# Latent-attention layer of a four-layer decoder trunk: weight units dealt in another order between the softmax steps, probability products half a step later

## The chip, the cores and the metric

The kernel runs as one program on one core of a Trainium2 chip. The metric is the device time of one execution in microseconds (us), the median of several runs. PE is the tensor engine, DVE the vector engine, ACT the scalar engine, POOL the GpSimd engine, SP the engine whose queue issues all DMAs here. Each engine works through its own instructions strictly in the order in which they stand, and semaphores hold one back until another is ready.

## What is computed

A trunk of four pre-norm residual layers over 1024 tokens of width 1024: gated linear attention, latent attention, stick-breaking attention, gated linear attention. The change touches the second one alone:

```python
def mla_mixer(h, w_in, q_norm_g, kv_norm_g, w_uq, w_ukv, w_out, cos, sin):
    proj = h @ w_in
    c_q, c_kv, k_rope, g = jnp.split(proj, [...], axis=-1)
    q = (rmsnorm(c_q, q_norm_g) @ w_uq).reshape(B, S, MLA_HEADS, MLA_NOPE + MLA_ROPE)
    q_nope, q_rope = jnp.split(q, [MLA_NOPE], axis=-1)
    q_rope = apply_rope(q_rope, cos[:, None, :], sin[:, None, :])
    kv = (rmsnorm(c_kv, kv_norm_g) @ w_ukv).reshape(B, S, MLA_HEADS, MLA_NOPE + MLA_V)
    k_nope, v = jnp.split(kv, [MLA_NOPE], axis=-1)
    for i in range(S // BLOCK_Q):          # 8 blocks of 128 queries, causal
        s = q_nope @ k_nope + q_rope @ k_rope
        p = softmax(where(causal, s * scale, -inf))
        outs.append(p @ v)
    return (o * jax.nn.silu(g)) @ w_out    # 16 heads of 128
```

## The kernel before, in words

Every float32 operand is held as two float16 halves (`_hi`, `_lo`), and each product takes three matmuls.

**The list of items.** `LatentAttention.build_items` writes one list; each engine runs through all of it and does its own share of each item. So the list is the order of every engine. Sixteen heads by eight query blocks give 128 steps, t = 8 h + i; block i looks at i + 1 blocks of 128 keys, so a score row is 128 wide at i = 0 and 1024 wide at i = 7. Item `s` t is the scores on PE (it waits until the exponential of t - 2 has left its pair of PSUM banks; at i = 0 also for `stacked`, the DMAs that laid out the rotary part of the queries, `mla_qr_stack`). `m` t is the row maximum and its negative on DVE and the exponential on ACT. `d` t is the reciprocal on DVE, the scaled copy `prob_halves` (high half) on ACT, the low half on DVE, and then on SP the DMA transpose of both. `pv` t is the product with the values on PE, which waits for that transpose; after every fourth one DVE multiplies by the gate (`mla_yt`), ACT and POOL split it (`mla_y_hi`, `mla_y_lo`).

**The filling.** Between these stand the units of the next projections; a unit fills one of three accumulators (PSUM banks 5, 6, 7 in turn) and must be emptied by DVE or ACT before the third unit after it starts. In columns of 128: `qn` 24, `kn` 12, `v` 12 (two each per head, emptied by ACT and DVE; "short" units), `qr` 24 (two for each pair of heads, before the even head; three DVE instructions each), `g` 96 (two per head; ACT and DVE also compute the SiLU) and `x` 48 (four per head from head 4 on, the output projection of the four heads before; DVE adds them to the residual). `g` and `x` are cut in four parts. Item `w` is the split of a weight slab into halves: ACT `w_hi`, then DVE `w_lo`, from one of two load buffers into one of three split buffers; `finish_items` decides where it stands. Item `rope` (POOL adds, ACT `st_hi`, DVE `st_lo`) finishes a rotary unit, and the `stage` items (SP, sixteen small DMAs for a pair of heads, four in each of four steps) lay it out as `mla_qr_stack` for the next even head.

**What sets the order.** A step of the list was: `s` t+1, `pv` t-1, `m` t+1, a first gap, `d` t+1, `stage` if any, a second gap. `weave` deals the filling into the gaps in equal shares of its own cost, whatever the attention work of the step. The order of the filling of one head h is: for odd h first the `qr` slab and units of the next pair, then `qn`, `kn`, `v` of head h+1 (with `rope` behind the `qn` units), then the `x` units, then the gate `g` of head h+1. The `stage` items stand in the steps i = 3 to 6 of the main list of the odd head, which puts the last of them just behind `d` of the head's last step.

## Time and profile before

| | us |
|---|---|
| runs (3) | 2726.56, 2728.34, 2731.05; median 2728.34 |
| profiled execution | 2728.8, of it 2726.8 from the first to the last instruction |
| PE busy | 2400.1 (88%) |
| DVE busy | 1523.5 (56%) |
| ACT busy | 1325.1 (49%) |
| mean granted TensorE clock | 0.953 |

The attention steps of the latent layer lie between 601 and 1442 us. A head's first step begins where DVE's row maximum has the form 128x128, which is how the stretches below were cut. "Idle before" is the time in which an engine had nothing to run just before an instruction, and the name behind the arrow is what released it.

### The profile page before, as it was taken

Reading aid. Unit: us, or ns where it says so; the run is one execution under the profiler, and the core shown is the slowest. Engines: PE = TensorE matmul, PEld = TensorE weight load, DVE = VectorE, ACT = ScalarE, POOL = GpSimd, SP = SyncE. Lnnn points to the kernel's source line nnn. Section 1 sums busy time; section 2 is a strip of 40 time slices with the busy share of each in tenths; the row PEclk is TensorE's granted clock in tenths of the full one; section 3 lists DMA queues with packets and bytes.
Section 4 is the critical chain, followed back from the end, with each engine's and each line's share of the span. In section 5 each row is a group of like instructions: output and inputs, shape, how many; then the busy total and the mean of one; then the engine's idle time right before and its main releaser. Section 6 shows DMA issues by size and latency. Waiting matters only on the chain. (4 is left out here: it accounts for less than half of the span.)

```text
span 2726.8 us, 42519 instructions
## 1 busy us (share of the span) xinstructions
PE 2400.1 (88%) x17068; PEld 1367.7 (50%) x17068; DVE 1523.5 (56%) x2164; ACT 1325.1 (49%) x1989; POOL 358.5 (13%) x266
## 2 busy tenths in 40 slices
PE   8999988977778878888787899999999899999987
PEld 4657753434444444444453455555554345775543
DVE  5555455665455455554556566666666474546554
ACT  4432333444444444444444477777777543334332
POOL 0000001121000000000002133222333210000001
PEclk9999999998889989999899999999999899999999
DMA  3011002213333332333332211111111121101013
GB/s 110 32 40 40 32 31 85 68 37 69 70 73 70 75 78 63 71 79 69 82 73 75 62 55 55 47 55 47 47 55 32 39 86 33 40 32 40 32 54 117
DMA packets 199767, 160.27 MB, mean 59 GB/s; under 512 B 160114, under 2 KB 165490, under 8 KB 199572
## 3 DMA queue, kind: packets, MB, share of 16 engines
q1 hardware_dynamic: 199572, 157.56, 21.7%
q8 instruction: 136, 2.23, 0.3%
q14 instruction: 59, 0.48, 0.1%
HBM read 98.79 MB, written 4.19 MB: 38 GB/s over the span
## 5 line engine op out<-in xcount | busy, mean ns | idle before, releaser
L222 PE MATMUL psum<-h_hi,w_hi 128*128 128x512 f16 x1128 | 431.6, 383 | 4.1 <-PEq L647 2.7
L223 PE MATMUL psum<-h_lo,w_hi 128*128 128x512 f16 x1128 | 431.1, 382 | 0.0
L224 PE MATMUL psum<-h_hi,w_lo 128*128 128x512 f16 x1128 | 430.7, 382 | 0.0
L2226 DVE SCALAR_TENSOR_TENSOR w_lo<-wf,w_hi 128x1024 f16<-128x1024 f32 (+3 forms) x194 | 232.3, 1200 | 188.8 <-ACT w_hi L2221 188.6
L238 PE MATMUL psum<-w_hi,h_hi 128*128 128x128 f16 x1504 | 256.9, 219 | 0.0
L239 PE MATMUL psum<-w_lo,h_hi 128*128 128x128 f16 x1504 | 256.6, 219 | 0.0
L240 PE MATMUL psum<-w_hi,h_lo 128*128 128x128 f16 x1504 | 256.6, 219 | 0.0
L1079 POOL TENSOR_TENSOR sb_al<-sb_zc,sb_ah 128x256 f16<-128x256 f32 (+2 forms) x96 | 166.3, 1732 | 372.0 <-ACT sb_ah L1044 372.0
L2221 ACT ACTIVATE w_hi<-wf 128x1024 f16<-128x1024 f32 (+3 forms) x194 | 188.4, 974 | 35.2 <-PE psum L224 16.3
L1578 ACT ACTIVATE ssum<-psum,mla_neg_top 128x128 f32<-128x128 f32 (+7 forms) x128 | 94.4, 738 | 207.7 <-DVE mla_neg_top L1487 207.7
L224 PEld LDWEIGHTS psum<-h_hi,w_lo 128*128 128x128 f16 x1128 | 111.2, 99 | 135.6 <-issue 4.7
L222 PEld LDWEIGHTS psum<-h_hi,w_hi 128*128 128x128 f16 x1128 | 111.2, 99 | 123.8 <-issue 12.3
L1499 DVE SCALAR_TENSOR_TENSOR mla_prob_halves<-ssum,mla_inv_total,mla_prob_halves 128x128 f16<-128x128 f32 (+7 forms) x128 | 104.7, 818 | 120.3 <-ACT mla_prob_halves L1586 120.3
L223 PEld LDWEIGHTS psum<-h_lo,w_hi 128*128 128x128 f16 x1128 | 111.1, 99 | 119.7 <-issue 6.3
L958 DVE TENSOR_TENSOR sb_Ll<-sb_Lf,sb_Lh 128x256 f16<-128x256 f32 (+2 forms) x96 | 96.8, 1008 | 111.4 <-ACT sb_Lh L1036 111.4
L238 PEld LDWEIGHTS psum<-w_hi,h_hi 128*128 128x128 f16 x1504 | 147.1, 98 | 18.3 <-issue 12.1
L239 PEld LDWEIGHTS psum<-w_lo,h_hi 128*128 128x128 f16 x1504 | 147.2, 98 | 6.0
L1586 ACT ACTIVATE mla_prob_halves<-ssum,mla_inv_total 128x128 f16<-128x128 f32 (+7 forms) x128 | 99.1, 774 | 104.5 <-DVE mla_inv_total L1496 104.5
L240 PEld LDWEIGHTS psum<-w_hi,h_lo 128*128 128x128 f16 x1504 | 147.2, 98 | 0.0
L1403 PE MATMUL psum<-mla_prob_halves_T,mla_v_hi 128*128 128x128 f16 x576 | 112.7, 231 | 38.8 <-DMA mla_prob_halves_T<-mla_prob_halves 37.5
L1638 POOL TENSOR_TENSOR mla_y_lo<-mla_yt,mla_y_hi 128x512 f16<-128x512 f32 x32 | 36.9, 1155 | 811.0 <-ACT mla_y_hi L1595 811.0
L1483 DVE TENSOR_REDUCE mla_top<-psum 128x1 f32<-128x128 f32 (+7 forms) x128 | 96.1, 750 | 61.3 <-PE psum L1388 60.5
(295 smaller groups left out, 5624.5 us busy)
## 6 DMA issues: line engine op xcount, KB each, us to landing
wf<-in_gla_out SPq DMA_DIRECT2D x32, 512.0 KB, 3.4
wf<-in_sb_in SPq DMA_DIRECT2D x32, 512.0 KB, 3.5
wf<-in_mla_out SPq DMA_DIRECT2D x20, 512.0 KB, 3.8
wf<-in_gla_v SPq DMA_DIRECT2D x16, 512.0 KB, 3.5
wf<-in_gla_g SPq DMA_DIRECT2D x16, 512.0 KB, 3.4
wf<-in_mla_gate SPq DMA_DIRECT2D x16, 512.0 KB, 3.5
wf<-in_sb_out SPq DMA_DIRECT2D x16, 512.0 KB, 3.5
xT<-in_x_T SPq DMA_DIRECT2D x16, 256.0 KB, 5.4
```

The lines of the kernel that those rows point to most:

```text
L222: pe.matmul(out, wh[:, w], act_hi[:, k, tok], start=(i == 0), stop=False)
L223: pe.matmul(out, wh[:, w], act_lo[:, k, tok], start=False, stop=False)
L224: mm = pe.matmul(out, wl[:, w], act_hi[:, k, tok], start=False, stop=(i == last))
L238: pe.matmul(out, act_hi[:, k, tok], wh[:, w], start=(i == 0), stop=False)
L239: pe.matmul(out, act_hi[:, k, tok], wl[:, w], start=False, stop=False)
L240: mm = pe.matmul(out, act_lo[:, k, tok], wh[:, w], start=False, stop=(i == last))
L1079: pool.tensor_tensor(self.al[s % 2][:, :, off:HALF], self.zc[s % 4][:, :, off:HALF], self.ah[s % 2][:, :, off:HALF], ALU.subtract).then_in ...
L1403: pe.matmul(out, vh, hi, start=(j == 0), stop=False)
L1499: dve.scalar_tensor_tensor(out=ph[:, w:2 * w], in0=self.prob[:, 0:w], scalar=self.inv_total[:, k], in1=ph[:, 0:w], op0=ALU.mult, op1=ALU.s ...
L1586: act.activation(self.ph[t % 2][:, 0:w], self.prob[:, 0:w], ACT.Copy, scale=self.inv_total[:, t % 4:t % 4 + 1]).then_inc(self.ph_ready, 1)
L2221: act.activation(self.w_hi[s % Layer.NSPLIT][:, 0:cols], self.wf[s % Layer.NLOAD][:, 0:cols], ACT.Copy, scale=W_SCALE).then_inc(self.w_hi_ ...
L2226: dve.scalar_tensor_tensor(out=self.w_lo[s % Layer.NSPLIT][:, 0:cols], in0=self.wf[s % Layer.NLOAD][:, 0:cols], scalar=W_SCALE, in1=self.w ...
```

## The change

The same units, matmuls and elementwise instructions, in another order:

- In a step, `m` t+1 and the first gap now stand ahead of `pv` t-1: `s`, `m`, gap, `pv`, `d`, `stage`, gap.
- `weave_even` deals the filling so that attention work and filling together advance evenly over the gaps of a head; `pe_cost` now counts `s` and `pv`.
- The filling of a head is drawn from its slabs in the order of a string (`ORDER`): short units stand between the long `x` units, the `qr` units of the next pair stand in the even head among the gate's units, and their `rope` items one head later, behind the second and third unit of the odd head's filling.
- `stage` stands in the steps i = 2 to 5 of the main list, one step earlier.
- `split_early` covers all slabs from 4 on, so a `w` item stands as soon as its split buffer is free.

```diff
+def weave_even(main, filler, cost):
+
+    gaps = sum(item[1] for item in main if item[0] == "gap")
+    work = sum(cost(item) for item in main + filler)
+    out, k, weight, spent = [], 0, 0, 0
+    for item in main:
+        if item[0] != "gap":
+            out.append(item)
+            spent += cost(item)
+            continue
+        weight += item[1]
+        while k < len(filler) and spent * gaps < weight * work:
             out.append(filler[k])
             spent += cost(filler[k])
             k += 1
...
+    ORDER = "uxuxuxuuxugrgr", "uuuguugxrxxrx"
     def pe_cost(self, item):
 
+        if item[0] in ("s", "pv"):
+            return (5 if item[0] == "s" else 3) * (item[1] % TT + 1)
         if item[0] not in ("u", "part"):
             return 0
...
+        for i in order:
+            s, units = todo[i]
+            name, payload = units.pop(0)
+            out.append(L.add_unit(name, payload, s, self.ACC[len(L.units) % len(self.ACC)]))
...
+    def filling(self, h):
+
+
+        made = {}
+        if h + 1 < MLA_HEADS:
+            made["u"] = self.up_slab(h + 1)
+        if h >= self.GROUP:
+            made["x"] = self.out_slab(h // self.GROUP - 1, h % self.GROUP)
+        if 1 <= h < MLA_HEADS - 1:
+            made["g"] = self.gate_slab(h + 1)
+        if h % 2 == 0 and h + 2 < MLA_HEADS:
+            made["r"] = self.rope_slab(h // 2 + 1)
+        turns = [k for k in self.ORDER[h % self.GROUP == 0] if k in made]
+        names = sorted(made, key=turns.index)
+        items = self.add_units([made[k] for k in names], [names.index(k) for k in turns])
+        if h % 2 and h + 1 < MLA_HEADS:
+            at = [i for i, it in enumerate(items) if it[0] == "u"][1:3]
+            for c, i in reversed(list(enumerate(at))):
+                items.insert(i + 1, ("rope", 3 + h + c))
+        return items
...
-        L.split_early = range(4, 7)
+        L.split_early = range(4, 1000)
...
-                items += weave(main, L.cut(filler, ("x", "g")), self.pe_cost)
+                items += weave_even(main, L.cut(filler, ("x", "g")), self.pe_cost)
                 main, filler = [], []
-            main += [("s", t + 1)] if t < last else []
+            main += [("s", t + 1), ("m", t + 1), ("gap", 1)] if t < last else []
             main += [("pv", t - 1)] if t else []
-            main += [("m", t + 1), ("gap", 1), ("d", t + 1)] if t < last else []
-            if h % 2 and h + 1 < MLA_HEADS and 3 <= i < 7:
-                main += self.stage_items(h + 1, range(2 * i - 6, 2 * i - 4))
+            main += [("d", t + 1)] if t < last else []
+            if h % 2 and h + 1 < MLA_HEADS and 2 <= i < 6:
+                main += self.stage_items(h + 1, range(2 * i - 4, 2 * i - 2))
             main += [("gap", 1)]
```

How this moves instructions is seen at three places. First SP's queue at the end of head 5 (`prob_halves_T` is the transposed probabilities of a step, 128x16x128 that of the step with 1024 keys, `mla_qr_stack` the rotary rows of head 6, `wf` a weight load). Before:

```order
L1657 DMA_TRANSPOSE mla_prob_halves_T0<-mla_prob_halves0 128x14x128
L1670 DMA mla_qr_stack<-mla_st_hi 32x512
L1670 DMA mla_qr_stack<-mla_st_lo 32x512
L1670 DMA mla_qr_stack<-mla_st_hi 32x512
L1670 DMA mla_qr_stack<-mla_st_lo 32x512
L1657 DMA_TRANSPOSE mla_prob_halves_T1<-mla_prob_halves1 128x16x128
L1670 DMA mla_qr_stack<-mla_st_hi 32x512
L1670 DMA mla_qr_stack<-mla_st_lo 32x512
L1670 DMA mla_qr_stack<-mla_st_hi 32x512
L1670 DMA mla_qr_stack<-mla_st_lo 32x512
L2215 DMA wf0<-in_mla_q_rope 128x256
```

Now:

```order
L1704 DMA mla_qr_stack<-mla_st_lo 32x512
L1691 DMA_TRANSPOSE mla_prob_halves_T0<-mla_prob_halves0 128x14x128
L1704 DMA mla_qr_stack<-mla_st_hi 32x512
L1704 DMA mla_qr_stack<-mla_st_lo 32x512
L1704 DMA mla_qr_stack<-mla_st_hi 32x512
L1704 DMA mla_qr_stack<-mla_st_lo 32x512
L1691 DMA_TRANSPOSE mla_prob_halves_T1<-mla_prob_halves1 128x16x128
L2249 DMA wf1<-in_mla_up 128x512
```

The last four rotary DMAs have moved from behind the transpose of the head's last step to ahead of it.

Second DVE's instructions in the first step of head 5 (from the row maximum of its 128-wide block on; `mla_rt` are the products of a `qr` unit with sine and cosine). Before:

```order
L1483 TENSOR_REDUCE mla_top<-psum 128x1
L1487 TENSOR_SCALAR mla_neg_top<-mla_top 128x1
L2226 SCALAR_TENSOR_TENSOR w_lo2<-wf0,w_hi2 128x512
L1457 SCALAR_TENSOR_TENSOR mla_rt0<-psum,mla_cos 128x512
L1461 SCALAR_TENSOR_TENSOR mla_rt2<-psum,mla_sin 64x512 x2
L290 TENSOR_TENSOR mla_silu_g<-mla_silu_g,mla_gate_tmp1 128x512
L1457 SCALAR_TENSOR_TENSOR mla_rt1<-psum,mla_cos 128x512
L1461 SCALAR_TENSOR_TENSOR mla_rt3<-psum,mla_sin 64x512 x2
L1496 RECIPROCAL mla_inv_total<-mla_total 128x1
L1499 SCALAR_TENSOR_TENSOR mla_prob_halves0<-ssum,mla_inv_total,mla_prob_halves0 128x128
L2226 SCALAR_TENSOR_TENSOR w_lo0<-wf1,w_hi0 128x1024
L601 SCALAR_TENSOR_TENSOR mla_qn_lo<-psum,mla_qn_hi 128x512
```

Now:

```order
L562 SCALAR_TENSOR_TENSOR xT<-psum,xT 128x512
L2260 SCALAR_TENSOR_TENSOR w_lo0<-wf1,w_hi0 128x1024
L2260 SCALAR_TENSOR_TENSOR w_lo1<-wf0,w_hi1 128x1024
L1517 TENSOR_REDUCE mla_top<-psum 128x1
L1521 TENSOR_SCALAR mla_neg_top<-mla_top 128x1
L619 SCALAR_TENSOR_TENSOR mla_qn_lo<-psum,mla_qn_hi 128x512
L1530 RECIPROCAL mla_inv_total<-mla_total 128x1
L1533 SCALAR_TENSOR_TENSOR mla_prob_halves0<-ssum,mla_inv_total,mla_prob_halves0 128x128
L562 SCALAR_TENSOR_TENSOR xT<-psum,xT 128x512
```

The rotary products and the splits of the slabs that the next units need have left this step; two slab splits, the second of them of a slab used later, stand at the end of the step before it.

Third PE's instructions in the third step of head 5 (384 keys; `prob_halves_T` with `mla_v` is `pv`, here of one block; `mla_ckv` with `w` a short unit, `mla_y` with `w` a part of an `x` unit). Before:

```order
L1387 MATMUL psum<-mla_kr_hh,mla_qr_stack 128x384
L1388 MATMUL psum<-mla_kr_ll,mla_qr_stack 128x384
L1403 MATMUL psum<-mla_prob_halves_T0,mla_v_hi 128x128
L1404 MATMUL psum<-mla_prob_halves_T0,mla_v_lo 128x128
L1405 MATMUL psum<-mla_prob_halves_T0,mla_v_hi 128x128
L238 MATMUL psum<-w_hi2,mla_ckv_hi 128x128
```

Now:

```order
L1422 MATMUL psum<-mla_kr_ll,mla_qr_stack 128x384
L240 MATMUL psum<-mla_y_hi,w_hi0 128x512
L241 MATMUL psum<-mla_y_lo,w_hi0 128x512
L242 MATMUL psum<-mla_y_hi,w_lo0 128x512
L240 MATMUL psum<-mla_ckv_hi,w_hi2 128x512
L241 MATMUL psum<-mla_ckv_lo,w_hi2 128x512
L242 MATMUL psum<-mla_ckv_hi,w_lo2 128x512
L240 MATMUL psum<-mla_y_hi,w_hi0 128x512
L241 MATMUL psum<-mla_y_lo,w_hi0 128x512
L242 MATMUL psum<-mla_y_hi,w_lo0 128x512
L1437 MATMUL psum<-mla_prob_halves_T0,mla_v_hi 128x128
L1438 MATMUL psum<-mla_prob_halves_T0,mla_v_lo 128x128
```

Three pieces of filling now stand between the scores and the product with the values, where none stood.

## Rows read from the trace of the kernel before

**Rows 1.** Page, part 1: busy time of the engines, share of the span.

```profile
PE 2400.1 (88%) x17068; PEld 1367.7 (50%) x17068; DVE 1523.5 (56%) x2164; ACT 1325.1 (49%) x1989; POOL 358.5 (13%) x266
```

**Rows 2.** Waits of PE, 601 to 1442 us: total, times, longest.

```profile
PE psum L1382 <- DMA mla_qr_stack<-mla_st_lo: 62.0, 7, 10.4
PE psum L1403 <- DMA mla_prob_halves_T<-mla_prob_halves: 37.5, 24, 4.0
PE psum L222 <- DVE w_lo L2226: 29.6, 12, 3.7
PE psum L238 <- issue: 26.4, 8, 5.0
```

**Rows 3.** Busy time by stretch: heads 0-1, 2-3, 4-5, 6-7, 12-13, 14, 15.

```profile
core 0: us, PE busy (x) PEld busy (x) DVE busy (x) ACT busy (x) POOL busy (x), PEclk, DMA share, GB/s
601.30:693.70 92.40, 62.11 (x447) 36.28 (x446) 49.14 (x96) 43.06 (x80) 6.89 (x5) 0.87 0.37 73
693.70:793.40 99.70, 75.04 (x547) 43.48 (x546) 52.88 (x101) 47.38 (x87) 8.05 (x6) 0.89 0.34 74
793.40:906.50 113.10, 92.39 (x643) 52.76 (x642) 60.46 (x111) 49.77 (x89) 7.05 (x6) 0.92 0.34 72
906.50:1019.30 112.80, 92.31 (x643) 52.67 (x642) 60.47 (x111) 49.72 (x89) 7.05 (x6) 0.92 0.33 72
...
1244.60:1357.30 112.70, 92.33 (x644) 52.68 (x642) 60.49 (x112) 49.74 (x89) 7.05 (x6) 0.92 0.35 72
...
1357.30:1405.50 48.20, 45.61 (x340) 26.92 (x338) 27.68 (x52) 22.73 (x40) 2.31 (x2) 0.98 0.30 72
1405.50:1442.00 36.50, 26.38 (x212) 15.44 (x211) 19.31 (x41) 18.05 (x32) 2.31 (x2) 0.99 0.42 80
```

**Rows 4.** The same for head 6 alone, head 7 alone and head 0 alone.

```profile
906.50:954.80 48.30, 45.70 (x340) 26.95 (x339) 26.87 (x51) 22.10 (x40) 2.31 (x2) 0.97 0.29 58
954.80:1019.30 64.50, 46.61 (x305) 25.72 (x304) 33.60 (x61) 27.63 (x49) 4.74 (x4) 0.89 0.36 82
601.30:639.20 37.90, 22.97 (x189) 14.47 (x188) 19.71 (x43) 18.48 (x35) 1.16 (x1) 0.91 0.33 63
```

**Rows 5.** Heads 6-7, ACT's busy time: the exponential (L1578), then the scaled copy (L1586).

```profile
906.50:1019.30 112.80, 13.26 (x32) 0.92 0.33 72
...
906.50:1019.30 112.80, 12.38 (x16) 0.92 0.33 72
```

**Rows 6.** Timeline of DVE and SP's queue where head 5 ends: start, duration, [idle before].

```profile
897.88 1.28 DVE L1499 SCALAR_TENSOR_TENSOR mla_prob_halves<-ssum,mla_inv_total,mla_prob_halves 128x1024 f16<-128x1024 f32 x1 [1.22 <-ACT mla_prob_halves L1586]
...
906.52 0.29 DVE L1483 TENSOR_REDUCE mla_top<-psum 128x1 f32<-128x128 f32 x1 [6.42 <-PE psum L1388]
...
891.96 1.54 SPq L1657 DMA_TRANSPOSE mla_prob_halves_T<-mla_prob_halves  x1
...
899.20 1.98 SPq L1657 DMA_TRANSPOSE mla_prob_halves_T<-mla_prob_halves  x1
...
903.52 0.58 SPq L1670 DMA_DIRECT2D mla_qr_stack<-mla_st_lo  x1
```

**Rows 7.** Waits in head 6 (906.5 to 954.8 us) that end on PE.

```profile
DVE mla_top L1483 <- PE psum L1388: 7.1, 2, 6.4
...
ACT mla_qn_hi L594 <- PE psum L224: 2.6, 2, 1.9
...
DVE mla_yt L1509 <- PE psum L1405: 1.9, 1, 1.9
```

**Rows 8.** Timeline of DVE, first steps of head 7, and of PE, second step of head 5.

```profile
957.81 0.69 DVE L2226 SCALAR_TENSOR_TENSOR w_lo<-wf,w_hi 128x512 f16<-128x512 f32 x1 [2.50 <-ACT w_hi L2221]
...
971.31 1.07 DVE L1475 TENSOR_TENSOR mla_st_lo<-mla_rt,mla_st_hi 128x512 f16<-128x512 f32 x1 [3.29 <-ACT mla_st_hi L1568]
...
860.20 0.27 PE L238 MATMUL psum<-w_hi,mla_ckv_hi 128*128 128x128 f16 x1 [4.98 <-issue]
```

**Rows 9.** Waits of PE in head 15 (1405.5 to 1442 us).

```profile
PE psum L1403 <- DMA mla_prob_halves_T<-mla_prob_halves: 10.1, 6, 3.2
```

More of the change, by code:

```diff
@@ L1219, in add_slab @@
                 out.append(("gz", n))
-                later = [("g2", n)]
             elif name in ("qn", "kn", "v"):
@@ L1224, in add_slab @@
                 self.ropes.append((name[0], *payload))
-        return out + later
-    def gate_items(self, h):
-        return self.add_slab(self.w["gate"][h], 1024, [("g", (h, c)) for c in range(2)])
-    def head_items(self, h):
-        out = []
-        if h % 2 == 0:
-            out += self.add_slab(self.w["q_rope"][h // 2], 256, [("qr", (h // 2, c)) for c in range(2)])
-        for it in self.add_slab(self.w["up"][h], 512, [(n, (h, c)) for n in ("qn", "kn", "v") for c in range(2)]):
-            out.append(it)
-            if h % 2 == 0 and it[0] == "u":
-                name, payload = self.L.units[it[1]][:2]
-                if name == "qn":
-                    out.append(("rope", 2 + h + payload[1]))
-        return out
+        assert not any(units for _, units in todo)
@@ L1243, in stage_items @@
     def stage_items(self, h, quarters):
         return [("stage", 2 + h + i // 4, i % 4) for i in quarters]
-    def out_items(self, group, part, halves=range(2)):
-        final = group == MLA_HEADS // self.GROUP - 1
-        items = self.L.slab(self.w["out"][group * 4 + part], 1024,
-                            [("x", (2 * part + k, c, final, group)) for k in range(2) for c in halves], self.ACC)
-        self.group_end[group] = len(self.L.units)
-        return items
     def build_items(self):
```

54 lines of the change are left out of this document (33 added, 21 removed).

## The prediction

> **What bounds the kernel now.** I read the page's busy times first: PE has work for 88% of the span, DVE for 56%, ACT for 49% [rows 1]. In the latent layer that average hides two regimes, so the waits of PE come next [rows 2]. PE loses 62.0 us in seven waits for the rotary rows `mla_qr_stack`, 37.5 us for transposed probabilities, 29.6 us for `w_lo`, and 26.4 us in front of `v` units: about 155 us together. Then the stretches [rows 3]: from head 4 on a pair of heads is a pattern of 112.5 to 113.1 us that comes five times, 563.9 us in all. Inside a pair the two heads differ: head 6 takes 48.3 us, head 7 takes 64.5 us [rows 4], though PE is busy 45.7 and 46.6 us. The granted clock in a pair is 0.92, so some 8% of 112.7 us, 9 us, of PE's 92.3 us is work stretched at the lower of the two clock levels (1.2 instead of 2.4 GHz); at full rate the matmuls of a pair need 83 to 85 us. The reader is to see that PE has nearly 30 us of slack in a pair, and to ask which line of work will take it up.
>
> That line runs through DVE and ACT and is almost serial. The maximum of the next step stands on DVE behind the low half of this one, and between them ACT computes the exponential and the scaled copy while DVE waits. For a pair: DVE busy 60.5 us [rows 3], ACT's exponentials 13.3 and its copies 12.4 us [rows 5], sum 86.2 us. What else must be paid is read from head 6, the one with the fewest stalls: 26.9 us of DVE [rows 4] and half of ACT's 25.7, 12.8 us, make 39.7 of its 48.3 us. The rest, 8.6 us, is hand-overs, ACT's other work in the line, and 5.2 us in which ACT or DVE waited for PE (2.6 for a `qn` unit, 1.9 for the product behind `mla_yt`, 0.7 in `mla_top`, whose other wait of 6.4 us is that for head 6's rotary rows) [rows 7]. Without the waits for PE the rest is 3.4 us a head.
>
> **The change part by part.** Nothing is added or removed; the 60.5 us of DVE work of a pair stays 60.5 us, and so do the matmuls.
>
> *The rotary DMAs one step earlier.* In the last step of head 5 SP issues the transpose at 899.20, and only behind it the last four rotary DMAs, the last at 903.52; head 6's first maximum starts at 906.52, after DVE has stood idle 6.42 us [rows 6]. In the new order these four stand behind the transpose that was issued at 891.96 [rows 6], so they would land some 7 us earlier, about 899.3. DVE had ended the low half at 897.88 + 1.28 = 899.16 and then two gate instructions, so nothing of the 6.4 us is left. The sixteen DMAs of a pair are the same ones and keep SP just as long; they now delay the transpose behind them, which matters little since `pv` is late too. Worth: 6.4 us in each of five pairs, somewhat more in the two earlier ones (PE's seven waits are 62.0 us in all, the longest 10.4 [rows 2]). What is late next is DVE's line itself.
>
> *Short units between long ones, `w` early, rotary units in the even head.* In the first steps of head 7 DVE waits 2.50 us for `w_hi` and 3.29 us for `st_hi`, which waited for POOL, which waited for DVE's own products just before; in head 5 PE waits 4.98 us in front of a `v` unit whose accumulator these hold [rows 8]. The same pattern comes in every odd head from 5 on, and makes most of the difference of 64.5 and 48.3 us. In the new order the slab splits stand a step or more ahead, and the rotary units a head ahead of their `rope`, so each of these waits has a reason to go. The work itself does not: about 6.7 us of DVE (33.6 against 26.9 [rows 4]) that now lies in both heads.
>
> *Products half a step later.* The transpose gets half a step of filling as cover. From head 4 on PE's wait for it is about 1 us a head already; the 37.5 us [rows 2] lie in heads 0 to 3 and 15, where filling is scarce, 10.1 us of them in head 15 [rows 9]. There the gain on PE is mostly no gain in time, since DVE's line needs nearly the whole step. The cost: `mla_yt` and ACT's `mla_y_hi` now stand inside the line, ahead of the reciprocal and the copy, twice a head. A bound from below is nothing, and from above the 1.9 us wait of rows 7 for each; I take it as part of the rest below.
>
> *Steps of equal length for PE.* A full head has some 42 us of PE work, 5.2 us a step, whatever i. DVE's line is not equal: at i = 7 the copy and low half alone wait and run 1.22 + 1.28 us [rows 6], at i = 0 a few tenths. So the long steps have little spare for their share of other DVE work and PE will wait for the banks there.
>
> **The sum.** For a pair of the full kind the line takes 86.2 us plus twice the rest. With 3.4 us a head that is 93.0 us, with head 6's 8.6 us it is 103.4. The middle is 98.2; I take 99, a little above it, for the gate products inside the line and the uneven steps. Five pairs: 563.9 - 495 = 68.9 us saved. Heads 0-1, by the same rule: 49.1 + 25.7 = 74.8, plus 6.8 to 17.2, so 81.6 to 92.0, I take 87 of now 92.4: 5.4 us. Heads 2-3: 52.9 + 25.7 = 78.6, so 85.4 to 95.8, I take 90.5 of 99.7: 9.2 us. Head 14: 27.7 + 12.8 = 40.5, so 43.9 to 49.1, I take 46.5 of 48.2: 1.7 us. Head 15: now 36.5, I take 36.0: 0.5 us. Before head 0 and behind head 15 the order hardly changes: nothing. Together 85.7 us. The profiled execution took 2728.8 us, half a microsecond over the median of 2728.3; 2728.8 - 85.7 = 2643.1, against the median 2643.
>
> Ends: with every stretch at its lower bound 98.9 + 10.8 + 14.3 + 4.3 + 1.0 = 129.3 us are saved, 2599. With every one at its upper bound 46.9 + 0.4 + 3.9 - 0.9 = 50.3 us, 2678.
>
> **Rivals.** *PE becomes the bound.* If the other DVE work fits into the times in which DVE waits for ACT, a pair is bound by PE's 83 to 85 us, say 86: 133.9 us saved in five pairs, with 25 to 30 in the first four heads 2565 to 2570. For it: the DVE work alone is 60.5 us. Against it: the engines run their lists in order, and in head 6 that work stood in the line nearly in full. Chance 0.07.
>
> *Less than half.* The long steps overflow, or the rotary rows still come late, so that about 6.4 us of a pair comes back: then a pair takes 105 to 106, five save 34 to 39 us, the rest of the layer 5: about 2688. For it: two slab splits now stand together behind an i = 7 step, and with three accumulators PE stops at once when DVE is late in a run of short units. Against it: PE can be a step ahead in the scores. Chance 0.20.
>
> *Slower, by the clock.* If many small gaps replace the two large ones, the lower clock may be granted far more often. The matmuls of a pair need 84 us at full rate; at a mean clock of 0.75 they need 112, as long as now, and that is the point from which it decides; at 0.70 they need 120, 7 us more than now in five pairs and about 12 in the first heads, so near 2776. The rows speak against it: head 15 has 10.1 us of such gaps in six pieces [rows 9] and a clock of 0.99 [rows 3], head 0 is idle 15 of 37.9 us and still has 0.91 [rows 4]. A rule speaks for it: the Trainium skill, page "TensorE: Matmul & The Clock Gate", section "A second HAM failure mode: psum-queue depth-cycling", tells of a kernel that cycles through accumulator banks and idles briefly between groups of matmuls so often that the clock swings between its two rates. This kernel cycles three banks. By that rule a pair would come out at 112 or more where the sum has 99; by head 15's row the clock stays up. A second way to the same side is a wait that no row shows, of ACT for filling that PE has not yet done, with the copy queued behind it: it would have to cost 0.85 us in each of 16 steps to use up the 13.7 us of a pair. Chance of slower, both together, 0.09.
>
> **How the numbers follow.** Forecast (2599 to 2678) 0.59, less than half 0.20, PE-bound 0.07, slower 0.09, no change 0.05 (gains and losses that cancel). A measurement of this kernel can tell about 0.2%, 5.5 us, from no change. Faster by more than that: 0.59 + 0.20 + 0.07 = 0.86; within 0.05; slower 0.09. The range reaches from 2598 to 2692: it takes in the forecast's ends and most of the second case, and leaves out the PE-bound case and what is slower or the same.
>
> **What would show it.** In the changed profile no wait of PE for `mla_qr_stack` over 2 us, and no `w_lo` or `v` wait over 2 us, if these steps are right. A pair of heads at 99 us with DVE busy 60.5 us, and PE waiting in many pieces of 1 to 2 us for DVE or ACT, if the line through DVE bounds. A granted clock of 0.95 or more in a pair; under 0.85 the clock rival is at work. Heads 0 and 2 no shorter, perhaps longer than now by some 3 us (they get the `qr` units), heads 1 and 3 shorter by some 10. The forecast is wrong if a pair stays above 106 us: then I have overlooked a wait, most likely ACT's or DVE's for a filling unit in the first gap.

## The result, and the profile after

One letter has to be set right first: in the diff above, the second string of `ORDER` lacks a `u`; the kernel has `"uuuguuugxrxxrx"`.

The changed kernel takes 2665.16 us (median of four runs, 2664.72 to 2669.93), the kernel before, on the same chip, 2729.03 us (2726.56 to 2731.05). The ratio is 0.977, with a 95% interval of 0.9753 to 0.9787: some 64 us are gained. The prediction was 2643 us, in a range from 2598 to 2692. So the direction and the range held; 86 us were forecast, and a quarter of them is missing. The page after, the span and part 1:

```profile
span 2668.2 us, 42519 instructions
PE 2400.2 (90%) x17068; PEld 1361.1 (51%) x17068; DVE 1530.2 (57%) x2164; ACT 1322.1 (50%) x1989; POOL 361.3 (14%) x266
```

The work is the same [rows 1], but for 7 us more of DVE, to which the last section comes back. The span was 2726.8 us and is 58.6 us shorter. The profiled execution took 2669.9 us, 4.8 above the median of its kernel, so what the trace shows as gained is some 5 us less than the runs have. The waits of PE in the latent layer (600 to 1400 us; total, times, longest) answer [rows 2]. Lines have moved: L1416 is L1382 of before (scores), L1437 is L1403 (product with the values), L240 and L256 are L222 and L238 (units), L2260 is L2226 (`w_lo`).

```profile
PE psum L1437 <- DMA mla_prob_halves_T<-mla_prob_halves: 31.9, 23, 3.9
PE psum L1416 <- DMA mla_qr_stack<-mla_st_lo: 27.9, 7, 5.5
PE psum L240 <- issue: 13.4, 9, 2.6
PE psum L240 <- DVE w_lo L2260: 11.1, 3, 3.8
PE psum L240 <- DVE mla_kn_lo L619: 8.6, 3, 2.9
PE psum L1416 <- ACT mla_silu_g L285: 6.0, 1, 6.0
PE psum L256 <- issue: 4.5, 5, 1.2
```

The rotary rows need two corrections. One of the seven waits in their group, 3.6 us, lies ahead of head 0, where there was none before. And the 6.0 us that the view puts down to ACT stand in front of the first score of head 4:

```profile
781.89 0.26 PE L1416 MATMUL psum<-mla_kn_hi,mla_qn_hi 128*128 128x128 f16 x1 [6.04 <-ACT mla_silu_g L285]
```

That score starts 2.19 us after SP began to issue the last rotary DMA (779.70). At the six other head changes it is 2.17 to 2.23 us, so this is most likely the same wait, and ACT's instruction ended by chance in the same moment. The wait at the seven head changes has then fallen from 62.0 to 30.3 us, that for `w_lo` from 29.6 to 11.1, that in front of `v` units (L256) from 26.4 to 4.5; the one for transposed probabilities has hardly moved (37.5, now 31.9). The group `mla_kn_lo` has grown from 1.3 us. Then the stretches by pair of heads, 14 and 15 apart, cut at the same row maximum and with the same columns as in [rows 3]:

```profile
606.00:690.40 84.40, 61.56 (x452) 34.95 (x451) 49.67 (x96) 40.20 (x76) 6.62 (x5) 0.90 0.35 72
690.40:782.90 92.50, 73.98 (x545) 43.10 (x544) 54.93 (x101) 47.27 (x86) 7.83 (x6) 0.89 0.38 78
782.90:887.60 104.70, 93.19 (x643) 52.04 (x642) 61.16 (x113) 49.57 (x89) 7.84 (x6) 0.94 0.35 76
887.60:989.60 102.00, 92.38 (x641) 50.95 (x640) 60.73 (x112) 49.15 (x89) 7.84 (x6) 0.95 0.36 79
989.60:1094.90 105.30, 93.88 (x642) 52.40 (x641) 61.00 (x112) 49.37 (x89) 7.84 (x6) 0.94 0.35 77
1094.90:1195.70 100.80, 90.97 (x643) 51.26 (x642) 60.80 (x112) 49.15 (x89) 7.83 (x6) 0.97 0.38 81
1195.70:1299.90 104.20, 92.84 (x640) 52.07 (x639) 60.98 (x112) 49.37 (x89) 7.83 (x6) 0.94 0.38 82
1299.90:1347.20 47.30, 46.43 (x350) 27.00 (x349) 28.19 (x52) 24.39 (x43) 2.31 (x2) 0.99 0.41 84
1347.20:1382.70 35.50, 26.46 (x206) 15.63 (x204) 20.50 (x41) 16.50 (x30) 2.31 (x2) 0.96 0.42 93
```

This table is the result. The five pairs of the full kind took 563.9 us and take 517.0, 103.4 on average, where 99 was forecast. The term by term comparison, saved against forecast: five pairs 46.9 (68.9), heads 0-1 8.0 (5.4), heads 2-3 7.2 (9.2), head 14 0.9 (1.7), head 15 1.0 (0.5). And one term has the wrong sign: head 0 now begins at 606.0 instead of 601.3 us, 4.7 us later, where "nothing" was forecast. Together 59.3, which is the shorter span to within a microsecond.

The two heads of a pair have drawn together by less than one would think. Heads 6 and 7 took 48.3 and 64.5 us [rows 4]; now:

```profile
887.60:945.50 57.90, 54.54 (x371) 29.79 (x370) 32.88 (x61) 26.27 (x47) 5.52 (x4) 0.94 0.34 75
945.50:989.60 44.10, 37.84 (x272) 21.16 (x270) 27.84 (x52) 22.88 (x42) 2.31 (x2) 0.97 0.40 85
```

The even head has become the long one (the `qr` units and their products on DVE lie there now: 32.88 us of DVE, 54.54 of PE; DVE's share of the `rope` items stays in the odd head), and in it PE is busy for 94% of the time. That is a first sign that DVE's line is no longer alone at the bound.

**Did the rotary rows do what the sum said?** SP's queue where head 5 ends, to be read beside [rows 6]:

```profile
883.94 0.58 SPq L1704 DMA_DIRECT2D mla_qr_stack<-mla_st_lo  x1
885.59 1.73 SPq L1691 DMA_TRANSPOSE mla_prob_halves_T<-mla_prob_halves  x1
```

The last rotary DMA is issued before head 5's last transpose and not 4 us behind it. DVE and PE there:

```profile
884.28 1.28 DVE L1533 SCALAR_TENSOR_TENSOR mla_prob_halves<-ssum,mla_inv_total,mla_prob_halves 128x1024 f16<-128x1024 f32 x1 [1.22 <-ACT mla_prob_halves L1620]
885.48 1.22 DVE L2260 SCALAR_TENSOR_TENSOR w_lo<-wf,w_hi 128x1024 f16<-128x1024 f32 x1
...
887.55 0.28 DVE L1517 TENSOR_REDUCE mla_top<-psum 128x1 f32<-128x128 f32 x1
...
886.12 0.27 PE L1416 MATMUL psum<-mla_kn_hi,mla_qn_hi 128*128 128x128 f16 x1 [3.65 <-DMA mla_qr_stack<-mla_st_lo]
```

DVE goes from the low half through a slab split and two gate instructions to the first maximum of head 6 without a pause; the 6.42 us of [rows 6] are gone as forecast. But PE still stands 3.65 us before that score, up to 6.0 elsewhere, because in the changed order PE gets there sooner. On DVE that wait no longer shows; on PE it does.

### The profile page after: what moved, and what is told of

The parts are those of the page before. It is cut to its first block and busy times, and to the rows that moved or that the text cites. A ratio compares the mean times of both kernels' runs of the same rounds, so it can differ in the third digit from the quotient of the medians.

```text
span 2668.2 us, 42519 instructions
## 1 busy us (share of the span) xinstructions
PE 2400.2 (90%) x17068; PEld 1361.1 (51%) x17068; DVE 1530.2 (57%) x2164; ACT 1322.1 (50%) x1989; POOL 361.3 (14%) x266
## 5 line engine op out<-in xcount | busy, mean ns | idle before, releaser
L240 PE MATMUL psum<-h_hi,w_hi 128*128 128x512 f16 x1128 | 433.3, 384 | 11.3 <-DVE mla_kn_lo L619 8.6
L2260 DVE SCALAR_TENSOR_TENSOR w_lo<-wf,w_hi 128x1024 f16<-128x1024 f32 (+3 forms) x194 | 232.5, 1205 | 155.5 <-ACT w_hi L2255 155.2
L256 PE MATMUL psum<-w_hi,h_hi 128*128 128x128 f16 x1504 | 256.9, 219 | 0.0
L1533 DVE SCALAR_TENSOR_TENSOR mla_prob_halves<-ssum,mla_inv_total,mla_prob_halves 128x128 f16<-128x128 f32 (+7 forms) x128 | 116.4, 910 | 121.6 <-ACT mla_prob_halves L1620 121.6
L240 PEld LDWEIGHTS psum<-h_hi,w_hi 128*128 128x128 f16 x1128 | 111.5, 99 | 128.7 <-issue 20.7
L256 PEld LDWEIGHTS psum<-w_hi,h_hi 128*128 128x128 f16 x1504 | 147.1, 98 | 18.3 <-issue 12.1
L1437 PE MATMUL psum<-mla_prob_halves_T,mla_v_hi 128*128 128x128 f16 x576 | 110.5, 228 | 35.3 <-DMA mla_prob_halves_T<-mla_prob_halves 31.9
L1039 ACT ACTIVATE sb_Lf<-sb_zc 128x256 f32<-128x256 f32 (+2 forms) x96 | 80.8, 842 | 95.2 <-DVE sb_zc L970 95.2
```

Source lines behind the costliest of these rows:

```text
L240: pe.matmul(out, wh[:, w], act_hi[:, k, tok], start=(i == 0), stop=False)
L256: pe.matmul(out, act_hi[:, k, tok], wh[:, w], start=(i == 0), stop=False)
L1437: pe.matmul(out, vh, hi, start=(j == 0), stop=False)
L1533: dve.scalar_tensor_tensor(out=ph[:, w:2 * w], in0=self.prob[:, 0:w], scalar=self.inv_total[:, k], in1=ph[:, 0:w], op0=ALU.mult, op1=ALU.s ...
L2260: dve.scalar_tensor_tensor(out=self.w_lo[s % Layer.NSPLIT][:, 0:cols], in0=self.wf[s % Layer.NLOAD][:, 0:cols], scalar=W_SCALE, in1=self.w ...
```

## The experiments

Every variant was timed against the kernel before on the same chip. To compare it with the changed kernel, that one is put at 0.9766 (2665.16 / 2729.03) of the before of the same chip. Its own interval is about 0.0017 to either side, 4.7 us, and each variant has one of much the same size, so differences below 5 us or so are no finding, and up to 7 us they are not sure. The trace of the changed kernel is of an execution 4.8 us above its median, so beside it a variant's trace can look that much too fast. Unless said otherwise the edit is made in the changed kernel (`-`) and gives the variant (`+`). "Pairs" are heads 0-1, 2-3 and so on, cut as above.

### e1_stage_late: the rotary DMAs a step later again

```diff
-            if h % 2 and h + 1 < MLA_HEADS and 2 <= i < 6:
-                main += self.stage_items(h + 1, range(2 * i - 4, 2 * i - 2))
+            if h % 2 and h + 1 < MLA_HEADS and 3 <= i < 7:
+                main += self.stage_items(h + 1, range(2 * i - 6, 2 * i - 4))
```

> The changed kernel with one part undone: the rotary DMAs stand again in the steps i = 3 to 6. Theory (my term of the sum): DVE loses again 6.4 us at each of seven head changes, so about 45 us slower than the changed kernel's 2665, near 2710. Rival: in the changed kernel PE still waits 3.6 to 5.5 us for these rows at each change, 27.9 us in all, where before it was 62.0; if only PE's wait counts, the part is worth 62.0 - 27.9 = 34 us, near 2699. If it is hidden behind the other line of work by now, under 10 us.

Measured: 2712.12 us, ratio 0.9947 (0.9932 to 0.9962), 50 us more than the changed kernel. The pairs are 91.5, 100.5, 110.5, 106.8, 111.0, 107.0 and 111.2 us, so 5 to 8 more in each, 6.4 on average. PE's wait for the rotary rows:

```profile
PE psum L1416 <- DMA mla_qr_stack<-mla_st_lo: 78.6, 8, 13.5
```

The changed kernel has 33.9 us there, its group of 27.9 and the 6.0 of head 4. So the rotary wait has grown by 44.7 us, as much as the seven pairs together (44.5). The `stage` step is worth what the sum gave it, 6.4 us in a pair.

### e8_before_stage: that edit alone, in the kernel before

```diff
-            if h % 2 and h + 1 < MLA_HEADS and 3 <= i < 7:
-                main += self.stage_items(h + 1, range(2 * i - 6, 2 * i - 4))
+            if h % 2 and h + 1 < MLA_HEADS and 2 <= i < 6:
+                main += self.stage_items(h + 1, range(2 * i - 4, 2 * i - 2))
```

> The kernel before with this one part alone: the rotary DMAs one step earlier. Theory (my term): 6.4 us of DVE's idle time in each of seven head changes, 45 us or somewhat more, so 2675 to 2680 against 2725 in these runs. Rival: as in the changed kernel a wait of some 4 us stays at each change, and the part alone is worth 30 us or less.

Measured: 2690.54 us, ratio 0.9855 (0.984 to 0.987): 41 us saved by two numbers. That is 64% of what the whole change brings. In its waits the rotary group is down to a fifth, that for `w_lo` stands as it was (29.7), and "issue" in front of `v` units has grown from 26.4 us [rows 2]:

```profile
PE psum L238 <- issue: 33.8, 17, 5.3
...
PE psum L1382 <- DMA mla_qr_stack<-mla_st_lo: 12.6, 6, 4.9
```

### e4_old_split: weight splits late again

```diff
-        L.split_early = range(4, 1000)
+        L.split_early = range(4, 7)
```

> The changed kernel with slab splits only as early as before (early ones for slabs 4 to 6). Theory: the early splits cost 4.7 us before head 0, where ACT's split of a slab now stands between the two halves of the first gates, and save the waits for w_lo later (29.6 us before, 11.1 now): so -4.7 + about 18, near 2679. Rival: the order of the units alone spread the slabs enough, and the old splits are 0 to 5 us faster, near 2661.

Measured: 2701.84 us, ratio 0.991 (0.9893 to 0.9926), 40 us more. The stretch from a weight load that all kernels have at some 561 us (`wf<-in_mla_up`) to head 0 is back to 39.9 us, as in the kernel before; in the changed kernel it is 44.9. So the missed term before head 0 comes from the early splits, all of it. From head 6 on the pairs take 109 to 112 us.

```profile
PE psum L240 <- DVE w_lo L2260: 48.9, 10, 7.8
```

The dealt order needs the early splits. The likely reason is that with units of several slabs mixed more slabs are needed soon; no view here shows that by itself.

### e12_before_split: the early splits alone, in the kernel before

```diff
-        L.split_early = range(4, 7)
+        L.split_early = range(4, 1000)
```

> The kernel before with the early slab splits alone (slabs 4 on instead of 4 to 6). Theory: undoing this in the changed kernel cost about 38 us, because the slabs of short units, mixed with x units, are needed soon after their buffer is free; alone, with the units kind by kind, it saves PE's waits for w_lo (29.6 us) and part of those in front of v units, less the 5 us before head 0: 15 to 30 us faster, 2697 to 2712. Rival: it pays only together with the new order of the units, and alone is within 8 us of 2727, since the rotary slab and the short units' slab are then still consumed within one step.

Measured: 2720.45 us, ratio 0.998 (0.9971 to 0.999): 4 us saved by the edit that costs 40 us when it is undone. The waits say why:

```profile
PE psum L1382 <- DMA mla_qr_stack<-mla_st_lo: 69.5, 8, 12.8
PE psum L238 <- issue: 32.3, 9, 5.3
...
PE psum L222 <- issue: 21.3, 16, 2.2
```

The 29.6 us for `w_lo` [rows 2] are gone; PE now waits 7.5 us more for the rotary rows (3.6 of them ahead of head 0) and 16.7 more in its two "issue" groups (26.4 [rows 2], and 10.5 for L222). Head 0 begins 5 us later (606.3, 44.9 us after the same load), as in the changed kernel. Most of the time of the wait that was taken away was handed to the next ones.

### e2_pv_first: the product with the values ahead of the maximum again

```diff
-            main += [("s", t + 1), ("m", t + 1), ("gap", 1)] if t < last else []
+            main += [("s", t + 1)] if t < last else []
             main += [("pv", t - 1)] if t else []
-            main += [("d", t + 1)] if t < last else []
+            main += [("m", t + 1), ("gap", 1), ("d", t + 1)] if t < last else []
```

> The changed kernel with the product with the values again ahead of the maximum and the first gap. Theory: from head 4 on the transposes had cover already, and the gate product leaves the serial line through DVE and ACT again, so 0 to 10 us faster than 2665. Rival: the half step of cover is needed now that PE's steps are of equal length (short attention steps no longer have short filling), PE's waits for transposed probabilities, 31.9 us in the changed kernel, rise to over 50, and it is 10 to 25 us slower.

Measured: 2687.5 us, ratio 0.9859 (0.9844 to 0.9874), 26 us more. The theory, that `mla_yt` inside the line costs more than the cover is worth, falls. The pairs are 86.7, 95.6, 107.5, 102.8, 107.7, 102.8, 106.5.

```profile
PE psum L1437 <- DMA mla_prob_halves_T<-mla_prob_halves: 41.9, 25, 6.6
```

Against the changed kernel this group grows by 10.0 us, the one for the rotary rows by 4.5 (32.4). That is 14.5 us. From head 0's start to head 15's the two traces differ by 16.9 us and not by 26: 5.4 in heads 0 to 3, 10.3 in the five full pairs, 1.2 in head 14. The other 9 us are in the runs alone; half of them can be the changed kernel's slower profiled execution, the rest is not accounted for.

### e3_old_weave: filling dealt without regard to the attention work

```diff
-        if item[0] in ("s", "pv"):
-            return (5 if item[0] == "s" else 3) * (item[1] % TT + 1)
...
-                items += weave_even(main, L.cut(filler, ("x", "g")), self.pe_cost)
+                items += weave(main, L.cut(filler, ("x", "g")), self.pe_cost)
```

> The changed kernel with the old dealing: the same share of filling in each gap, whatever the attention work of the step. Theory (uneven steps): DVE's line needs 5.4 us and more in the steps of 1024 keys and 2 in those of 128, so equal steps for PE suit it worse than steps that grow with i, and the old dealing makes it 10 to 20 us faster than 2665. Rival: PE, busy 92 of 103 us in a pair, is the engine that is short of time, and dealing its work evenly saves it waits: the old dealing is 5 to 20 us slower.

Measured: 2673.79 us, ratio 0.9809 (0.9795 to 0.9824), 12 us more. The theory, that equal steps hurt DVE's uneven line and that the old dealing is faster, falls. The pairs are 88.1, 95.5, 103.2, 101.3, 103.4, 101.4, 103.4. Heads 0-3, where filling is scarce, take 6.6 us more. The five full pairs sum to 512.7, 4.3 us less than with equal steps; that is within the 4.8 us by which the changed kernel's trace is slow, and shows no gain.

### e6_rotary_odd: rotary units in the odd head again

```diff
-    ORDER = "uxuxuxuuxugrgr", "uuuguuugxrxxrx"
+    ORDER = "rruxuxuxuuxugg", "uuuguuugxxxx"
...
-        if h % 2 == 0 and h + 2 < MLA_HEADS:
-            made["r"] = self.rope_slab(h // 2 + 1)
+        if h % 2 and h + 1 < MLA_HEADS:
+            made["r"] = self.rope_slab((h + 1) // 2)
...
-            at = [i for i, it in enumerate(items) if it[0] == "u"][1:3]
+            at = [i for i, it in enumerate(items) if it[0] == "u"][2:4]
```

> The changed kernel with the qr units again at the head of the odd head's filling, with their rope items two units behind them, all else as changed. Theory: the chain DVE, POOL, ACT, DVE stands again inside two steps (3.3 us of wait before), and the odd head gets 4.6 us more DVE work while the even one loses it: 8 us a pair for five pairs, 35 to 45 us slower. Rival: the work only moves between the heads of a pair and the pair's sum hardly changes: within 10 us of 2662.

Measured: 2665.95 us, ratio 0.9768 (0.9752 to 0.9784), the same as the changed kernel. The theory gave this placement 35 to 45 us and falls: the two heads of a pair come out more alike (52.2 and 52.2 instead of 57.8 and 46.4 in the changed kernel, heads 12 and 13), but their sum stays (104.4 against 104.2). Moving the rotary units to the even head is worth nothing that can be told.

### e5_one_kind: units of one kind together

```diff
-    ORDER = "uxuxuxuuxugrgr", "uuuguuugxrxxrx"
+    ORDER = "uuuuuuxxxxgrgr", "uuuuuuxxxxgrgr"
```

> The changed kernel with the filling drawn kind by kind (six short units, then four x units, then gates, with the qr units among the gates of the even head as changed). Theory: short units in a row make PE wait for accumulators and DVE's line carry six splits in two steps; mixing them was worth 10 to 20 us, so 2672 to 2682. Rival: the early slab splits and the moved rotary units had removed those waits already, and the order of kinds is worth under 4 us.

Measured: 2694.84 us, ratio 0.9874 (0.9854 to 0.9893), 27 us more. But the edit did a second thing. In heads 4, 8 and 12 the `x` units now stand ahead of the gate's, and need the last rows of the head just finished. PE waits for POOL:

```profile
PE psum L240 <- POOL mla_y_lo L1672: 17.8, 3, 5.9
```

These three heads take 66.2, 65.1 and 65.6 us instead of 58.1, 58.9 and 57.8: 22 of the 33 us by which the two traces differ. The profiled execution of this variant was itself 8 us above its median. In the pairs without such a head mixing is worth 2.8 (6-7) and 4.9 us (10-11). So the order within a head is worth a few microseconds a pair and no more; the run is blurred by its second effect.

### e10_light_rotary: less work on DVE

One of the three DVE products of each rotary unit of the pairs behind the first is left out, so the rotary part of these queries is computed only in part.

```diff
-                for lo in (0, MLA_ROPE):
+                for lo in ((0, MLA_ROPE) if name == "kr" or r < 4 else (0,)):
```

> The changed kernel with one of the three DVE products of each rotary unit of the pairs 1 to 7 left out (half of the crossed rotary product is missing, so what is computed is not the reference's). It takes 14 x 0.69 = 9.7 us of work from DVE and nothing from PE. Theory (the serial line through DVE bounds): 8 to 10 us faster than the changed kernel. Rival (PE, busy 92 of 103 us in a pair, bounds where it is not waiting, and DVE has slack in those steps): 0 to 3 us.

Measured: 2661.21 us, ratio 0.9753 (0.9732 to 0.9773), 2 us less, which is within the error. Fourteen products of 0.69 us, 9.7 us of DVE, were taken from the line. By the medians the time did not follow, as the rival had it. But the intervals of the two ratios (0.9732 to 0.9773, and 0.9753 to 0.9787) also leave room for the theory's 8 us, and in the traces the stretch from head 0's start to head 15's is 733.0 us against 741.2, 8.2 less, of which up to 4.8 can be the changed kernel's slower execution. So this run does not decide between theory and rival.

### e7_stage_early: the rotary DMAs another step earlier

```diff
-            if h % 2 and h + 1 < MLA_HEADS and 2 <= i < 6:
-                main += self.stage_items(h + 1, range(2 * i - 4, 2 * i - 2))
+            if h % 2 and h + 1 < MLA_HEADS and 1 <= i < 5:
+                main += self.stage_items(h + 1, range(2 * i - 2, 2 * i))
```

> The changed kernel with the rotary DMAs one step earlier still (i = 1 to 4). Theory: PE's remaining wait of 3.6 to 5.5 us in each of seven head changes (27.9 us in all) goes, and with it the lower clock behind it; the step after it waits for PE now (3.5 us for a qn unit), so 15 to 30 us faster, 2632 to 2647. Rival: DVE's line sets the pace there (its maximum of the new head comes without a wait), and the gain is under 5 us.

Measured: 2660.33 us, ratio 0.9739 (0.9725 to 0.9754), 7 us less than the changed kernel; the two intervals just touch, so it is a likely gain and no sure one. Between theory and rival. The rotary wait at the head changes is gone but for 2.3 us (the longest of the three below is the one ahead of head 0), and two others have grown out of it:

```profile
PE psum L240 <- issue: 22.7, 15, 3.2
PE psum L240 <- DVE mla_qn_lo L619: 11.7, 3, 4.1
...
PE psum L1416 <- DMA mla_qr_stack<-mla_st_lo: 5.9, 3, 3.6
```

28.0 us less for the rotary rows (22.0 in their group, and the 6.0 of head 4), 11.7 more for `mla_qn_lo` and 9.3 more on "issue". By pairs only 6-7 and 10-11 gain (102.0 and 100.8 become 97.5 each); the pairs that begin with head 4, 8 or 12 do not (105.7, 105.1, 105.9).

### e9_gate_apart: the gate's units apart in every fourth head

In heads 4, 8 and 12 the third step stood out, with 11 us. ACT, DVE and PE there in the changed kernel, head 8 (ACT's first gate function began at 1006.09):

```profile
1008.49 0.63 ACT L291 ACTIVATE mla_gate_tmp<-mla_gate_tmp 128x512 f32<-128x512 f32 x1
1009.03 0.58 ACT L612 ACTIVATE mla_kn_hi<-psum 128x512 f16<-128x512 f32 x1
...
1009.64 0.69 DVE L619 SCALAR_TENSOR_TENSOR mla_kn_lo<-psum,mla_kn_hi 128x512 f16<-128x512 f32 x1 [2.50 <-ACT mla_kn_hi L612]
1010.48 0.38 PE L240 MATMUL psum<-h_hi,w_hi 128*128 128x512 f16 x1 [2.87 <-DVE mla_kn_lo L619]
```

A gate unit is followed by short units. ACT first works through the SiLU of the gate, then empties the short ones, and PE runs out of accumulators: 2.50 us on DVE, 2.87 us on PE.

```diff
-    ORDER = "uxuxuxuuxugrgr", "uuuguuugxrxxrx"
+    ORDER = "uxuxuxuuxugrgr", "uuuuuugxrxxgrx"
```

> The changed kernel with another string for the heads 4, 8 and 12: the six short units first, then gate unit, x, rotary, x, x, gate unit, rotary, x, so that no gate unit stands between short ones. Theory: the 11.2 to 11.3 us that the third step of each of these heads takes (ACT's three gate functions stand ahead of its split of a kn unit, DVE waits 2.5 us for that, PE 2.9 and 1.2 us) shrinks to 6 or 7, so 4 us in each of three heads, 12 us together, and 2655 where the changed kernel is at 2667 in runs like these. Rival: the time comes back as the same line's work in the next steps, under 4 us.

Measured: 2664.32 us (2657.67 to 2665.23), ratio 0.9761 (0.9742 to 0.9781): no difference that can be told. In the profiled execution heads 4, 8 and 12 do shrink (54.4, 55.1, 55.2 us) and the `mla_kn_lo` group is gone, but the `w_lo` group has grown from 11.1 to 17.0 us. The five full pairs sum to 510.3 us against 517.0, 6.7 less, of which up to 4.8 can be the changed kernel's slower execution. Read alone, this experiment says nothing.

### e11_all: the last two together, and late splits before head 0

```diff
-    ORDER = "uxuxuxuuxugrgr", "uuuguuugxrxxrx"
+    ORDER = "uxuxuxuuxugrgr", "uuuuuugxrxxgrx"
...
-        L.split_early = range(4, 1000)
+        L.split_early = (4, 5, 6, *range(11, 1000))
...
-            if h % 2 and h + 1 < MLA_HEADS and 2 <= i < 6:
-                main += self.stage_items(h + 1, range(2 * i - 4, 2 * i - 2))
+            if h % 2 and h + 1 < MLA_HEADS and 1 <= i < 5:
+                main += self.stage_items(h + 1, range(2 * i - 2, 2 * i))
```

> The changed kernel with three edits: rotary DMAs in the steps i = 1 to 4, the string of the run before for heads 4, 8 and 12, and early slab splits for slabs 4 to 6 and from 11 on, but not for 7 to 10. Theory: 8 (measured for the first alone) + 0 to 12 (the second) + 5 us (the gates before head 0 as before), so 13 to 25 us faster than the changed kernel, 2642 to 2654. Rival: the edits share one slack, and together they give no more than 10.

Measured: 2644.39 us (2643.66 to 2646.16), ratio 0.9695 (0.9679 to 0.971). That is 19 us less than the changed kernel, and it is the fastest of all. Head 0 begins at 597.8 us, 8.2 earlier than in the changed kernel. Of that 3.5 us arose before the latent layer, where nothing was changed, and 4.7 are the late splits: the stretch from the `wf<-in_mla_up` load to head 0 is 40.2 us and not 44.9. So the parts by themselves would give 12 us (7 of e7, nothing of e9, 5 of the splits). That 19 is more than their sum is likely, but with errors of some 5 us in each it is not sure. Its pair 6-7:

```profile
875.90:973.40 97.50, 89.56 (x637) 50.36 (x635) 60.67 (x112) 49.06 (x90) 7.82 (x6) 0.98 0.38 83
```

In it PE is busy for 92% of the time, in pair 8-9 (101.2 us) for 91%. The five full pairs sum to 500.0, 100.0 each.

## Why the prediction was right, and where its sizes were off

**What bounds the layer.** The reading was that PE has nearly 30 us of slack in a pair and DVE's line sets the time. Of before that is true: the waits of DVE and PE at the rotary rows and splits were real, and their removal gave the gain. Of after it is half true. The text put PE's need at 83 to 85 us a pair. Summed over the 641 matmuls of pair 6-7, at the spacing that neighbours show at the upper clock level (0.21 to 0.22 us for 512 columns, 0.055 for 128), it is an estimated 87 us. To that come 3 to 6 us for work at the lower level, so PE needs 90 to 93 of the 102 to 105 us that a pair takes. Each of the two engines waits for the other for short times. That neither alone is the bound is an argument from these numbers; e10, which could have shown it from the other side, does not decide it.

**The rotary DMAs, 6.4 us a pair.** Right in mechanism and size: undone 50 us (e1), alone 41 us (e8), where the working gives 32 for five pairs and "somewhat more" for the others. The statement that no wait of PE for `mla_qr_stack` over 2 us would be left is wrong. All seven head changes keep one, of 3.6 to 6.0 us, 4.3 on average, since PE now arrives sooner; an eighth, of 3.6 us, is new ahead of head 0. The landing was worked out rightly from [rows 6]; that the one who waits would also move was not considered.

**Short units, `w` early, rotary units ahead.** The waits of [rows 8] went, as forecast: those for `w_lo` from 29.6 to 11.1, those before `v` units from 26.4 to 4.5. That no `w_lo` wait over 2 us would be left is wrong: three of up to 3.8 us are. The share of the parts was wrong too. The rotary placement is worth nothing that can be told (e6), mixing 3 to 5 us in the two pairs that can be compared (e5), and the early splits are worth 40 us, but only in this order (e4, e12).

**Products half a step later.** The text saw no gain in time and a cost between 0 and 1.9 us. e2 measured 26 us for it, 17 of them in the traces. The step that failed is that from head 4 on there is nothing left to cover, and that in the other heads "the gain on PE is mostly no gain in time, since DVE's line needs nearly the whole step". In the traces 10.3 us come from the five full pairs and 5.4 from heads 0 to 3. That PE, which needs some 90% of a pair, can no longer make up for such waits fits this, but is not shown by itself.

**The pair, 99 us forecast and 103.4 measured.** This is the term that was mis-sized, by 4.4 us in five pairs. That is 22 of the 26 us by which the trace falls short of the sum (85.7 against 59.3); the start of head 0 is 4.7 of it, and the other terms nearly cancel. The sum was DVE 60.5, exponentials and copies 25.7, and twice a rest between 3.4 and 8.6 us. The first two stand: DVE 60.73 to 61.16 us, against 60.5. The rest did not shrink. For pair 6-7 it is (102.0 - 60.7 - 25.7) / 2 = 7.8 us a head, for pair 8-9 (105.3 - 61.0 - 25.7) / 2 = 9.3: head 6 of before all over. The largest waits that end on PE, heads 6 to 9 (887.6 to 1094.9 us), to be read beside [rows 7]:

```profile
DVE mla_top L1517 <- PE psum L1422: 6.6, 6, 2.3
ACT mla_qn_hi L612 <- PE psum L242: 5.3, 2, 3.5
...
DVE mla_yt L1543 <- PE psum L1439: 4.7, 2, 3.3
...
DVE xT L562 <- PE psum L242: 3.6, 3, 1.7
```

With two of 0.6 and 0.5 us behind these they are 21.3 us in four heads, 5.3 a head. Head 6 had 5.2. The middle of the two bounds was taken on the unspoken ground that some of these waits would go; nothing in the rows spoke for that. The upper bound, 103.4 by the text, was met to the decimal, by some luck.

**Heads 0 to 3, 14 and 15.** 17.1 us against 16.8, with single terms off by up to 2.6 us. The shape was right as well: head 0 and 2 are 3.4 and 5.8 us longer (some 3 were named), heads 1 and 3 are 11.5 and 12.9 us shorter (some 10).

**Before head 0, nothing.** Wrong: head 0 begins 4.7 us later, and measured from the `wf<-in_mla_up` load at 561 us it is 5.0 (44.9 against 39.9). `split_early` covers the slabs ahead of head 0 as well. A `w` item holds a weight load on SP too, and this load waits until its buffer is free. The load of a gate slab now stands ahead of the sixteen rotary DMAs of head 0 in SP's queue, and waits for the split that DVE ends at 592.85. SP's queue and PE's first score, now:

```profile
592.87 0.33 SPq L2249 DMA_DIRECT2D wf<-in_mla_gate  x1
593.25 0.63 SPq L1704 DMA_DIRECT2D mla_qr_stack<-mla_st_hi  x1
...
602.78 0.59 SPq L1704 DMA_DIRECT2D mla_qr_stack<-mla_st_lo  x1
...
605.13 0.27 PE L1416 MATMUL psum<-mla_kn_hi,mla_qn_hi 128*128 128x128 f16 x1 [3.62 <-DMA mla_qr_stack<-mla_st_lo]
```

Before, the first of the sixteen was issued at 587.18, the last at 597.25, and PE began that score at 600.08 without a wait. With the late splits of e4 the order on SP is the old one and the 5.0 us are back; e12 has the delay in the kernel before, with a wait of 3.64 us at the same place. A change to a rule that places items acts wherever the rule does, and on every engine that takes part in an item; this stretch was passed over.

**The rivals.** PE as the bound did not come, yet the real case lies nearer to it than the text had it, since its 83 to 85 us were too low. "Less than half" took a pair at 105 to 106 us; two of the five reach 104.7 and 105.3, the mean does not. The clock went the other way: from the table above, the time at the lower level is 2 x (1 - clock) x length, summed 95 us, against 139 by [rows 3] for the same heads (with the 0.92 of the full pairs). The rule weighed in the prediction (the Trainium skill, page "TensorE: Matmul & The Clock Gate", section "A second HAM failure mode: psum-queue depth-cycling") would have had the clock swing more often. The trace does not agree: 0.94 to 0.97 in the full pairs, and 0.90 and 0.89 in heads 0-1 and 2-3 (0.87 and 0.89 before), with three banks in turn.

**The parts do not add up.** Undone one at a time, `stage` costs 50 us, the splits 40, the product's place 26, the dealing 12: 128 us of a change that brings 64. Alone, `stage` brings 41 and the splits 4. A part can remove one of several waits that stand in a row, and is then worth its length only if the next one has gone as well. For the splits e12 shows this in its waits. Which part covers which, pair by pair, is not settled.

## What to carry to other kernels

When engines run one shared list, work out what each engine needs at full rate before calling one of them the bound; if the second one needs some 85% of the stretch, as here, do not expect the small waits to shrink, and take the upper end of the rest. That is the lesson of one case. When data come a step earlier, the engine that used them may come earlier too and wait for them anew. An item that holds a load can keep back all DMAs behind it in the same queue. Judge the parts of a reordering by undoing them in the final version and by making them alone: here one edit was worth 4 us in the one and 40 in the other, and two edits without a sure effect of their own were part of a 19 us gain.

## What the runs showed of the hardware

DVE's low-half instruction (L1499 before, L1533 after, two inputs in SBUF) became slower without any change to it. The groups of before and of after, 128 instructions each, busy time and mean:

```profile
L1499 DVE SCALAR_TENSOR_TENSOR mla_prob_halves<-ssum,mla_inv_total,mla_prob_halves 128x128 f16<-128x128 f32 (+7 forms) x128 | 104.7, 818 | 120.3 <-ACT mla_prob_halves L1586 120.3
L1533 DVE SCALAR_TENSOR_TENSOR mla_prob_halves<-ssum,mla_inv_total,mla_prob_halves 128x128 f16<-128x128 f32 (+7 forms) x128 | 116.4, 910 | 121.6 <-ACT mla_prob_halves L1620 121.6
```

11.7 us more. It sits in two of the eight widths. One before, then two after, with POOL beside them:

```profile
919.48 0.49 DVE L1499 SCALAR_TENSOR_TENSOR mla_prob_halves<-ssum,mla_inv_total,mla_prob_halves 128x256 f16<-128x256 f32 x1 [0.58 <-ACT mla_prob_halves L1586]
...
1003.38 1.16 POOL L1672 TENSOR_TENSOR mla_y_lo<-mla_yt,mla_y_hi 128x512 f16<-128x512 f32 x1 [27.74 <-ACT mla_y_hi L1629]
1003.74 1.08 DVE L1533 SCALAR_TENSOR_TENSOR mla_prob_halves<-ssum,mla_inv_total,mla_prob_halves 128x256 f16<-128x256 f32 x1 [1.03 <-ACT mla_prob_halves L1620]
...
1031.74 1.19 DVE L1533 SCALAR_TENSOR_TENSOR mla_prob_halves<-ssum,mla_inv_total,mla_prob_halves 128x768 f16<-128x768 f32 x1 [1.18 <-ACT mla_prob_halves L1620]
1032.08 1.99 POOL L1661 TENSOR_TENSOR mla_rt<-mla_rt 128x512 f32<-128x512 f32 x1
1040.39 1.27 POOL L1661 TENSOR_TENSOR mla_rt<-mla_rt 128x512 f32<-128x512 f32 x1 [6.33 <-DVE mla_rt L1495]
```

The same form takes 0.49 us with POOL idle and 1.08 with `mla_y_lo` beside it. It works both ways: POOL's addition, 1.27 us alone, takes 1.99 when it begins while DVE's instruction runs, 0.72 us more, and DVE has 0.85 us left at that point (1032.93 - 1032.08). With the product ahead of the maximum (e2), `mla_y_lo` falls elsewhere, and the group is back at 106.8 us and a mean of 834 ns. So the moved product brings about 10 us of extra DVE time, and is worth 26 us in spite of it. What it would be worth with POOL's instruction out of the way was not tried.

The Trainium skill, page "SBUF — State Buffer", section "SBUF: two separate sides", has a rule for this: DVE and GpSimd share one pair of ports, and whichever of them starts first holds it for the whole instruction, a DVE instruction with two inputs in SBUF among them. The trace agrees on POOL's side (0.72 us against the 0.85 left). On DVE's side the two 1.08 and 1.19 us are somewhat shorter than a full block would make them; spans on POOL are rough.
